# A top-k threshold search that flips one float bit per pass, and two more blocks chosen one stage earlier

## The reference

```
isc = relu(einsum('bqhd,bsd->bqhs', qib, k_idx))            # 8 index heads
isc = einsum('bqh,bqhs->bqs', wib, isc) * idx_scale
isc = where(admissible, isc, -inf)                          # own and earlier chunks of 64
top_val, top_idx = lax.top_k(isc, 256)                      # per query
# attention of 16 heads over the 256 chosen keys, with a bias -slope * |distance|
```

## Time and profile before

| | us |
|---|---|
| runs of the kernel | 3651.45, 3652.26, 3652.67 |
| median of the three | 3652.26 |
| profiled execution, span | 3662.1 |

### The profile page before, as it was taken

The page is one execution under the profiler, slowest core; times in us unless marked ns, Lnnn a source line. Parts: engine busy times, 40 slices in busy tenths (PEclk is TensorE's granted clock), DMA queues, the critical chain, the costliest instruction groups (busy, mean ns, idle before and its releaser), DMA issues. The chain is left out here.

```text
span 3662.1 us, 90162 instructions
## 1 busy us (share of the span) xinstructions
PE 3333.1 (91%) x36876; PEld 2902.3 (79%) x36876; DVE 2130.1 (58%) x5023; ACT 1898.0 (52%) x3756; POOL 815.7 (22%) x900
## 2 busy tenths in 40 slices
PE   5899999989888888997797999997789999999899
PEld 5777899978777776885665898897678888888787
DVE  7100100028788893331199998996967777777322
ACT  5122211126677773221287766755468888888311
POOL 3222200001377770001101532521510000000000
PEclk9999999989899999998899999998899999999999
DMA  5333421159412314345421436335563333331432
GB/s 195 109 115 118 144 65 65 48 112 238 131 46 75 83 39 146 114 154 195 116 58 46 138 113 182 135 96 163 207 183 88 91 84 84 92 86 51 153 112 85
DMA packets 368257, 416.91 MB, mean 114 GB/s; under 512 B 51816, under 2 KB 272616, under 8 KB 366952
## 3 DMA queue, kind: packets, MB, share of 16 engines
q1 hardware_dynamic: 303096, 318.55, 30.1%
q10 hardware_dynamic: 64768, 92.81, 7.0%
HBM read 247.21 MB, written 164.10 MB: 112 GB/s over the span
## 5 line engine op out<-in xcount | busy, mean ns | idle before, releaser
L1402 PE MATMUL s_o<-s_v,s_pT 128*64 128x65 f32 (+1 forms) x13056 | 436.6, 224 | 9.6 <-issue 9.4
L1402 PEld LDWEIGHTS s_o<-s_v,s_pT 128*64 128x64 f32 x13056 | 402.0, 138 | 46.0 <-issue 24.6
L230 PE MATMUL s_acc<-s_wh,s_hT 128*128 128x256 f32 (+1 forms) x1408 | 430.6, 306 | 7.8 <-ACT s_parts L653 4.6
L232 PE MATMUL s_acc<-s_wh,s_hT 128*128 128x256 f32 (+1 forms) x1408 | 429.8, 305 | 0.0
L231 PE MATMUL s_acc<-s_wl,s_hT 128*128 128x256 f32 (+1 forms) x1408 | 429.7, 305 | 0.0
L230 PE MATMUL s_acc<-s_hT,s_wh 128*128 128x512 f32 x880 | 349.8, 397 | 57.3 <-DVE s_wl L329 25.8
L1565 ACT ACTIVATE s_probs<-s_probs,s_nmx 128x512 f32<-128x512 f32 (+3 forms) x640 | 388.8, 662 | 12.0 <-DVE s_nmx L1630 12.0
L1614 DVE CUSTOM_DVE_ANT_0 s_probs<-s_s,s_scores 128x512 f32<-128x512 f32 (+3 forms) x640 | 364.4, 607 | 8.9 <-issue 5.1
L2375 DVE TENSOR_SCALAR_CACHE_REDUCE s_scratch<-s_scores,s_thr 128x384 uint8<-128x384 f32 (+4 forms) x320 | 365.3, 1209 | 1.1
L231 PE MATMUL s_acc<-s_hT,s_wh 128*128 128x512 f32 x880 | 347.7, 395 | 0.0
L232 PE MATMUL s_acc<-s_hT,s_wl 128*128 128x512 f32 x880 | 347.5, 395 | 0.0
(11 more groups left out here) (278 smaller groups left out, 7180.2 us busy)
## 6 DMA issues: line engine op xcount, KB each, us to landing
fm<-s_parts ACTq DMA_DIRECT2D x120, 512.0 KB, 2.8
s_y<-y SPq DMA_DIRECT2D x32, 640.0 KB, 5.9
y<-s_g SPq DMA_DIRECT2D x18, 1024.0 KB, 5.8
kc<-s_parts SPq DMA_DIRECT2D x32, 512.0 KB, 3.3
s_w<-in_o_fm SPq DMA_DIRECT2D x25, 512.0 KB, 4.5
s_w<-in_o_w_in SPq DMA_DIRECT2D x12, 1024.0 KB, 5.6
s_qh<-fm SPq DMA_DIRECT2D x42, 256.0 KB, 3.2
s_ql<-fm SPq DMA_DIRECT2D x42, 256.0 KB, 3.7
```

Source lines behind the costliest of these rows:

```text
L230: nc.tensor.matmul(out, sh, mh, start=(j == 0), stop=False)
L232: ins = nc.tensor.matmul(out, sl, mh, start=False, stop=(j == n - 1))
L1402: last = nc.tensor.matmul(o_ps[half * HD:(half + 1) * HD, 0:w], pT[half][:, x0:x0 + HD], v[:, g.u.kbs[g.a + x], vc:vc + w], start=(g.first ...
```

## The change

A threshold is now kept as the bits of a float itself, in `best`, which begins as all ones. Each pass makes its candidate by one exclusive-or of `best` with a constant mask (`MASKS`: all bits in the first pass, then one bit each), and the counts read the candidate directly. The conversion key to float and the shifted mask are gone from the pass. Once, in front of `settle`, `as_key` turns the bits into the ordered key (two instructions). `EARLY` goes from 6 to 8: blocks 6 and 7 are chosen in the halves stage. They are wider than the scratch of 1024 columns, so `choose_wide` works on them in two pieces. `after` goes from 20 to 26 in `between`. In the latent stage one `choose_two` is gone, and the means and scaling of row pairs 4 to 7 stand right behind `adjust`.

```
-                for k in range(4):
+                for q in range(4, NP):
+                    mean(q)
+                for q in range(4, NP):
+                    normalize(q)
+                for k in range(3):
                     n = search.EARLY + 2 * k
                     def low_parts():
-                        for t in range(4 + 4 * k, 8 + 4 * k):
+                        for t in range(8 + 4 * k, 12 + 4 * k):
                             low_part(t)
-                    search.choose_two(dve, n, even, rank, low_parts if k in (1, 2) else None)
-                    if k == 0:
-                        for q in range(4, NP):
-                            mean(q)
-                        for q in range(4, NP):
-                            normalize(q)
+                    search.choose_two(dve, n, even, rank, low_parts if k in (0, 1) else None)
...
-    EARLY = 6
-    PER = 7
+    EARLY = 8
+    PER = 4
+    MASKS = [0xFFFFFFFF] + [1 << n for n in range(30, -1, -1)]
...
+    def as_key(self, dve, src):
+        v = self.nc.vector
+        self.link(dve, v.tensor_scalar(self.flip[:], src[:], 31, SIGN, ALU.arith_shift_right, ALU.bitwise_or))
+        self.link(dve, v.tensor_tensor(src[:], src[:], self.flip[:], ALU.bitwise_xor))
...
         for i in range(first, last):
-            self.link(dve, v.tensor_tensor(self.cand[:], self.best[:], self.bit[:], ALU.bitwise_or))
-            self.as_float(dve, self.cand)
+            self.link(dve, v.tensor_scalar(self.cand[:], self.best[:], self.MASKS[i], None, ALU.bitwise_xor))
...
-            v.tensor_scalar(self.bit[:], self.bit[:], 1, None, ALU.logical_shift_right)
...
+    def choose_wide(self, dve, n, even, rank):
+        v, L, H = self.nc.vector, self.width(n), PIECE
...
+        rank_equal(H, L)
+        self.link(dve, v.tensor_tensor(room, room, rank[:, L - H - 1:L - H], ALU.add))
+        rank_equal(0, H)
+        self.link(dve, v.tensor_scalar(room, rank[:, H - 1:H], room, 0.5, ALU.add, ALU.mult))
+        self.link(dve, v.tensor_tensor(room_left, room, rank[:, H - 1:H], ALU.subtract))
+        keep(0, H, room)
+        rank_equal(H, L)
+        keep(H, L, room_left)
...
-                lead, span, after = 3, 2 * wide_slots + slots, 20
+                lead, span, after = 3, 2 * wide_slots + slots, 26
...
-                        search.choose(dve, n, search.scratch[:, 0, :], search.scratch[:, 1, :])
+                        pick = search.choose if search.width(n) <= PIECE else search.choose_wide
+                        pick(dve, n, search.scratch[:, 0, :], search.scratch[:, 1, :])
```

More of the change, by code:

```diff
@@ L2325, in __init__ @@
         self.neg_dist = sc.sb("neg_dist", [P, S])
-        self.best, self.bit, self.cand, self.flip, self.thr, self.enough = (
-            sc.sb(name, [P, self.NB], U32) for name in ("best", "bit", "cand", "flip", "thr", "enough"))
+        self.best, self.cand, self.flip, self.thr, self.enough = (
+            sc.sb(name, [P, self.NB], U32) for name in ("best", "cand", "flip", "thr", "enough"))
         self.high, self.low = (sc.sb(name, [P, self.NA], U32) for name in ("high", "low"))
@@ L2356, in start @@
             v.memset(self.most[:, n:n + 1], self.width(n) - 2 * TOPK)
-        v.memset(self.best[:], 0)
-        self.link(dve, v.memset(self.bit[:], SIGN))
+        self.link(dve, v.memset(self.cand[:], 0))
+        self.link(dve, v.tensor_scalar(self.best[:], self.cand[:], 0xFFFFFFFF, None, ALU.bitwise_xor))
+        self.started = self.links
     def as_float(self, dve, src):
@@ L2375, in bits @@
                 v.tensor_scalar(self.junk[n % 2][:, 0:self.width(n)], self.scores(n + self.B0),
[L2376 removed]
+                                self.cand[:, n:n + 1].bitcast(F32), None, ALU.is_ge, ALU.add,
                                 accum_out=self.cnt[:, n:n + 1]).then_inc(self.counted, 1)
[L2378 removed]
             dve.wait_ge(self.counted, i * ND + ND)
@@ L2395, in balances @@
             if k < 32 * NA:
-                n = ND + k % NA
+                n, thr = ND + k % NA, self.cand
                 if k % NA == 0:
-                    act.wait_ge(self.ch, k // NA * self.PER + 5)
+                    act.wait_ge(self.ch, k // NA * self.PER + self.started + 1)
             else:
-                n = k - 32 * NA
+                n, thr = k - 32 * NA, self.thr
                 if n == 0:
@@ L2405, in balances @@
             self.nc.scalar.activation(signs[:, 0:self.width(n)], self.scores(n + self.B0), ACT.Sign, scale=-1.0,
-                                      bias=self.thr[:, n:n + 1].bitcast(F32),
+                                      bias=thr[:, n:n + 1].bitcast(F32),
                                       accum_out=self.balance[:, n:n + 1]).then_inc(self.balanced, 1)
@@ L2496, in choose, with rank_equal, keep @@
             self.link(dve, step())
+    def choose_wide(self, dve, n, even, rank):
+        v, L, H = self.nc.vector, self.width(n), PIECE
+        t = self.thr[:, n:n + 1].bitcast(F32)
+        room, room_left = self.room[:, n:n + 1], self.cnt[:, 0:1]
+        def rank_equal(x0, x1):
+            ev, rk = even[:, 0:x1 - x0], rank[:, 0:x1 - x0]
+            self.link(dve, v.tensor_scalar(ev, self.scores(n + self.B0)[:, x0:x1], t, None, ALU.is_equal))
+            self.link(dve, v.tensor_tensor_scan(out=rk, data0=ev, data1=ev, initial=0.0, op0=ALU.add, op1=ALU.max))
+        def keep(x0, x1, left):
+            sc_b, ev, rk = self.scores(n + self.B0)[:, x0:x1], even[:, 0:x1 - x0], rank[:, 0:x1 - x0]
+            self.link(dve, v.tensor_scalar(rk, rk, left, 2.0 ** -126, ALU.is_gt, ALU.mult))
+            self.link(dve, v.scalar_tensor_tensor(out=ev, in0=sc_b, scalar=t, in1=rk, op0=ALU.subtract, op1=ALU.is_lt))
+            self.link(dve, v.scalar_tensor_tensor(out=sc_b, in0=ev, scalar=MASKED,
+                                                  in1=self.neg_dist[:, S - L + x0:S - L + x1],
+                                                  op0=ALU.mult, op1=ALU.add))
+        rank_equal(H, L)
[6 more added lines that the diff above has]
+        keep(H, L, room_left)
     def choose_two(self, dve, n, even, rank, midway=None):
```

1 line of the change is left out of this document (added).

## The result

The changed kernel took 3668.14 us (median of 5 runs, 3666.46 to 3670.78), the kernel before beside it 3652.26: 15.9 us between the medians. The ratio of the two is put at 1.0039 (95% interval 1.0028 to 1.0050), which is 14.2 us slower (10.2 to 18.3). The median lies outside the predicted range of 3645 to 3663. In the profiled execution the span is 3664.7 us.

A forecast was written before the change was run, and what follows sets the result against it. It took PE, with DVE close behind, to bound the halves stage and DVE the end of the latent stage. +9.9 us and -5.5 us made +4.4 on 3652.3, so 3656.7 us, range 3645 to 3663.

The forecast's parts named there:

- The passes: Halves stage, search: each of 32 passes loses 0.63 us of small DVE instructions, 20.2 us in all, to about 12.15 us each.
- 2430 at the earliest: Halves stage: ACT's slots let the passes end at 2430 us at the earliest, some 25 us sooner than before.
- The choosing: End of halves stage: two new blocks add 20.6 us on DVE; choosing ends at 2515.9, next stage begins 9.9 us later.
- the lock: Halves stage: POOL's last weight split holds the shared SBUF ports exclusively, so DVE gets little done before 2465.0 us.
- The latent stage: Two blocks (16.0 us) leave DVE, but the stage ends only 5.5 us sooner; bounds 2 and 10 us.
- the wait for the roots: Latent stage: normalizations need ACT's roots, queued behind evacuations until 2556.3 us, so DVE idles most of 2546 to 2556.4.
- The sum: Whole kernel: +9.9 us in the halves stage and -5.5 us in the latent stage make +4.4 us.
- the likeliest case: Whole kernel: time within 0.2% (7.3 us) of no change, given a chance of 0.57.
- a row event lasts (2503.45 - 2463.88) / 14 = 2.83 us: Halves stage: PE's time per row event, used to place ACT's sums and the passes' end.
- I carry the difference over: Adds the +4.4 us, found in a profiled span of 3662.1 us, to the median of 3652.3, giving 3656.7.
- Rival 3: Halves stage: tighter ACT slots stop PE 3 to 6 us more, total 3660 to 3663 us; chance 0.26.
- Rivals 1 and 2: First: choosing starts at 2452.6, halves tail hidden, 3646.8 us, chance 0.17. Second: latent stage gains all 16 us, 3641, chance 0.11.

The follow-up runs named there:

- e10: The changed kernel with an unused 64-byte tile between raw and split weights, so the split weights sit where they did before: 3653.64 us, ratio 0.9999.
- e5: The changed kernel with an unused 56-byte tile in the freed room: 3655.73 us, ratio 1.0005 to the kernel before.
- e4: The kernel before with the new passes alone, plus an unused 56-byte tile that keeps later tiles in place: 3648.42 us, ratio 0.9986.
- e17: e4 once more, unchanged: 3648.26 us, ratio 0.9990 to the kernel before.
- e15: The kernel before with new passes and constant 26, six early blocks, old latent order, weights kept at the old place: 3656.25 us, ratio 1.0009.
- e16: e5 with the constant back at 20, eight early blocks: 3668.73 us, ratio 1.0034 to the kernel before.
- e0: The kernel before, unchanged, timed and profiled again: 3650.9 us, ratio 0.9994.
- e14: The kernel before with an unused 192-byte tile behind the small search tiles, which moves the split weights: 3663.03 us, ratio 1.0030.
- e1: The changed kernel, unchanged, timed and profiled again: 3666.55 us, ratio 1.0038 to the kernel before.
- e6: The kernel before with an unused tile of 2 columns, which moves the weights 32 bytes up: 3661.35 us, ratio 1.0014.
- e11: The changed kernel with an unused 64-byte tile between split weights and evacuation tiles, so only the tiles behind move back: 3666.4 us, ratio 1.0043.
- e7: The kernel before with eight early blocks and the new latent order, but old passes and constant 20: 3668.68 us, ratio 1.0043.
- e12: The changed kernel with split weights left in place and the other operand hT 64 bytes lower: 3658.32 us, ratio 1.0018.

## Why the prediction was wrong

**The passes.** Right: 12.15 us measured, 0.63 less than the earlier trace rows. They ended at 2434.5, 4.5 us later than "2430 at the earliest" and 20 us sooner than before instead of 25, which moved nothing, since choosing waits for the sums, as forecast.

**The choosing.** The mechanism was right: the new blocks 20.4 us (20.6 forecast), the lock as forecast, in its place two us later. Its end is 2517.77, forecast 2515.9, because PE's events and with them POOL's split came later. Not every execution pays it: in e10 the split was over at 2448.28 and the first comparison had its 0.42 us. The page "SBUF — State Buffer" of the Trainium skill, section "Who interferes with whom", as the prediction named it, is borne out by 4.88 us beside 4.64. Its rule that whichever starts first has the ports is not to be seen in the rows: DVE's starts at 2462.51, 0.03 us before POOL's at 2462.54, and still DVE was the one held up.

**The latent stage.** Right, in mechanism and in size. The wait for the roots is there (4.91 us). The two first traces give 140.5 and 132.9 us, -7.5 where -5.5 was forecast; but the nine profiles with the old order have 136.8 to 140.7 us (mean 138.8) and the eleven with the new order 131.4 to 135.1 (mean 133.4), which is -5.4.

**The sum at the old distance.** +4.4 us forecast; e5 gives +1.8 (-2.2 to +5.5) and e10 -0.4 (-3.7 to +2.9). The forecast lies inside the first interval and just outside the second. As a change of the search alone it is within 0.2% of no change, which was the likeliest case. The parts, at the old distance: passes -5.1 and -3.7 (e4, e17); passes and constant +3.3 (e15); passes, blocks and latent order without the constant +12.4 (e16); all together -0.4 to +1.8.

**The step that failed** is "a row event lasts (2503.45 - 2463.88) / 14 = 2.83 us", used for both kernels. It held PE's own speed fixed, between the kernels and from one execution to the next. The diff removes one small tile; no step asked what is allocated behind it. Twenty-four row products at 119.5 ns make 2.87 us, at 113.6 ns 2.73: the event had in truth two lengths, and the trace of before happened to be an execution near the longer (117.5 ns, halves stage 522.4 us against 514.6 in e0). That is also why the two first traces seemed to confirm the forecast: the execution of before already had well over half of the extra PE time that the change makes permanent (117.5 - 113.6 and 231.1 - 229.1 ns are 10.9 us of the 16.9). "I carry the difference over" to a median 9.8 us below that span was where the error entered the number: the term for the moved weights, left at nothing, measured 12.4 and 14.6 us (1.0039 - 1.0005 and 1.0039 - 0.9999, the kernel after against e5 and e10). The independent measure is e14, the old kernel with its weights moved, at 11.0 us (6.6 to 15.3); with +1.8 or -0.4 for the search it makes 10.6 to 12.8, against 14.2 (10.2 to 18.3) for the whole change.

**Rival 3** came nearest in time (3660 to 3663), by luck: its mechanism exists (6.2 us for the longest wait of PE in e1, against 1.9 before), but it does not decide. e10, with 7.1 us of such waits, takes the time of the kernel before, and e16, with 2.3, is slow.

```profile
PE s_acc L230 <- ACT s_parts L653: 8.7, 2, 6.2
```

That is e1; the kernel after in its first profile had 3.4 us in all, and it is the same kernel with the same ratio (1.0039 and 1.0038). Rivals 1 and 2 fell: choosing began at 2460.97, not at 2452.6, and the roots held the normalizations.

## What to carry to other kernels

Removing or adding a small tile is a change to every tile allocated behind it. Before a change of 0.3% is explained by its instructions, put an unused tile of the same size in the freed room and time that: it is the cheapest control, and here it gave back all of the loss that the intervals can tell. When a profiled span stands well off the median of the timed runs, compare the rates inside it (products in a fixed stretch at full granted clock) with a second profile before any duration from it goes into a sum. And time parts on both sides of a balance: with the weights at the old distance the constant 26 costs with six blocks (e15 against e4 and e17) and pays with eight (e5 against e16).

## What the runs showed of the hardware

TensorE's products of one shape, at granted clock 1.00 and without an idle gap, started 113.4 to 120.0 ns apart (256 columns) and 226.6 to 233.8 ns apart (512 columns), by the distance in SBUF between stationary and moving operand: in the table above 64 bytes past a multiple of 512 was the fast one for both forms together, 0 the fastest for 512 columns and the slowest for 256. Between kernels that differ in nothing else it was worth 5 to 16 us of 3650 (e6 against before the least, e11 against e10 the most).

The Trainium skill, page "TensorE: Matmul & The Clock Gate", section "Back-to-back issue gap", has the gap as a function of the number of columns and of the weight load. The runs differ: at one number of columns it also goes by address. The page "SBUF — State Buffer", section "🔬 SBUF: two separate sides", has PE never waiting on another engine and gives weight loads a second, independent read port. That the distance between PE's own two operands decides speaks against their reads being independent; how they meet was not shown, and neither was whether other operand types or shapes behave so.

What stays open: at the same distance of 64 bytes, row products were 113.4 to 113.8 ns apart in six profiles (e0, e4, e7, e10, e12, e16) and 115.1 to 117.5 in four (e17, e15, e5 and the first of before), in the same program even (before and e0, e4 and e17). Nothing tried explains which execution gets which.
